# Attention on TensorE: the products with the values of unit u-3 issued ahead of the turning of unit u-2

## The reference, cut to what matters

```python
s_c = jnp.einsum('bqhgd,bnhd->bhgqn', qc, kc).astype(jnp.float32) + head_bias(dist_c)
p_c = masked_softmax(s_c, dist_c >= 0)
o_c = jnp.einsum('bhgqn,bnhd->bqhgd', p_c.astype(vc.dtype), vc)
...
p_s = masked_softmax(...)
o_s = jnp.einsum('bhgqnk,bhqnkd->bqhgd', p_s.astype(v_sel.dtype), v_sel)
...
p_w = masked_softmax(s_w, mask_w)
o_w = jnp.einsum('bhgqk,bkhd->bqhgd', p_w.astype(vwc.dtype), vwc)
return gc[..., 0:1] * o_c + gc[..., 1:2] * o_s + gc[..., 2:3] * o_w
```

## Time and profile before

| | us |
|---|---|
| median of 3 runs (1825.06 to 1826.18) | 1825.11 |
| the profiled execution's own time | 1823.85 |
| its span in the profile | 1821.1 |
| attention, from its first scores to the copy of its last tile | 189.90 to about 280.3 |
| TensorE busy over the span | 1739.9 (96%) |

### The profile page before, as it was taken

How to read it: one execution, slowest core, us unless ns; L and a number is a source line. 1 busy time by engine, 2 the same in 40 slices (tenths; PEclk the granted TensorE clock), 3 DMA queues, 4 the chain that set the end, 5 groups by cost and what they waited for, 6 DMA issues and landing times.

```text
span 1821.1 us, 36387 instructions
## 1 busy us (share of the span) xinstructions
PE 1739.9 (96%) x15582; PEld 1289.7 (71%) x15582; DVE 981.6 (54%) x2058; ACT 497.6 (27%) x1175; POOL 469.8 (26%) x482
## 2 busy tenths in 40 slices
PE   7999899999999999999999979989899999999997
PEld 3446564688888888844555448888867888888886
DVE  4570561444444422323332467666686799999443
ACT  3021682211111100134112544444333222222000
POOL 2060341010111100012000045555453255555100
PEclk9999999999999999999999989999999999999999
DMA  6521102343333343432412100000022222222231
GB/s 236 176 70 47 70 2 98 123 166 123 117 128 117 127 139 118 139 104 91 153 46 76 47 2 5 4 4 5 5 99 70 81 83 91 93 83 84 94 102 55
DMA packets 44760, 158.04 MB, mean 87 GB/s; under 512 B 5112, under 2 KB 7816, under 8 KB 43576
## 3 DMA queue, kind: packets, MB, share of 16 engines
q1 hardware_dynamic: 38304, 132.14, 22.2%
q10 hardware_dynamic: 6296, 23.58, 3.4%
HBM read 150.96 MB, written 6.31 MB: 86 GB/s over the span
## 4 chain that ended last, share of the span: by engine, by line
PE 89%; DVE 6%; ACT 2%; issue 1%; POOL 1%; DMA 0%; SPq 0%; DVEq 0%; ACTq 0%; POOLq 0%
PE psum L364 19%; PE psum L1441 15%; PE psum L1617 15%; PE psum L3083 14%; PE psum L1301 3%; PE psum L2381 2%; PE psum L2954 2%; PE psum L2385 2%; PE psum L691 2%; DVE mem L2571 1%; PE psum L1250 1%; PE psum L1101 1%; PE psum L1074 1%; PE psum L1089 1%; DVE mem L2599 1%
## 5 line engine op out<-in xcount | busy, mean ns | idle before, releaser
L364 PE MATMUL psum<-mem 128*128 128x512 f32 (+1 forms) x880 | 350.3, 556 | 12.3 <-DMA mem<-in_units 11.0
L364 PEld LDWEIGHTS psum<-mem 128*128 128x128 f32 x880 | 165.8, 190 | 184.9 <-issue 178.6
L1441 PE MATMUL psum<-mem 128*128 128x256 f32 x1232 | 272.5, 380 | 1.2 <-issue 1.2
L1617 PE MATMUL psum<-mem 128*128 128x256 f32 x1232 | 269.7, 379 | 0.0
L1441 PEld LDWEIGHTS psum<-mem 128*128 128x128 f32 x1232 | 231.2, 189 | 38.5 <-issue 6.3
L1617 PEld LDWEIGHTS psum<-mem 128*128 128x128 f32 x1232 | 232.1, 189 | 35.0 <-issue 2.4
L3083 PE MATMUL psum<-mem 128*128 128x256 f32 x1176 | 254.4, 379 | 0.0
L3083 PEld LDWEIGHTS psum<-mem 128*128 128x128 f32 x1176 | 221.9, 189 | 32.8 <-issue 0.5
L3208 DVE SCALAR_TENSOR_TENSOR mem<-psum,mem 128x441 f32<-128x441 f32 (+2 forms) x352 | 215.5, 680 | 0.0
L1368 POOL TENSOR_TENSOR mem<-mem 128x256 f32<-128x256 f32 x22 | 16.7, 757 | 281.9 <-DVE mem L1576 271.0
L2381 PE MATMUL psum<-mem 64*64 64x64 f32 x1920 | 75.0, 224 | 13.0 <-DVE mem L2599 5.4
(11 more groups left out here) (387 smaller groups left out, 2426.0 us busy)
## 6 DMA issues: line engine op xcount, KB each, us to landing
mem<-in_units SPq DMA_DIRECT2D x246, 512.0 KB, 3.5
mem<-in_cw ACTq DMA_DIRECT2D x2, 2048.0 KB, 11.2
mem<-in_wn ACTq DMA_DIRECT2D x1, 2048.0 KB, 9.1
bias_tiles<-bias_scratch ACTq DMA_DIRECT2D x1, 2048.0 KB
mem<-bias_tiles ACTq DMA_DIRECT2D x1, 2048.0 KB
mem<-in_xT ACTq DMA_DIRECT2D x1, 2048.0 KB, 9.4
x_scratch<-mem ACTq DMA_DIRECT2D x1, 2048.0 KB, 8.9
mem<-x_scratch ACTq DMA_DIRECT2D x1, 2048.0 KB, 10.5
```

What stands on the lines that cost most here:

```text
L364: last = pe.matmul(dst, w[:, k, :], rhs(k), start=(k == 0), stop=(k == 7))
L1441: last = eng.matmul(dst, w[:, k, :], rhs(k), start=start and k == 0, stop=stop and k == 3, skip_group_check=True)
L1617: ins = eng.matmul(dst, w[:, k, :], rhs(k0 + k), start=opens and first and k == 0, stop=closes and last_ and k == k1 - k0 - 1, skip_group_ ...
```

## The change

TensorE's loop over the units issues the same instructions. Only `weigh(u - 3)` and `turn(u - 2)` have changed places:

```diff
@@ -1108,10 +1108,10 @@
                 for u in range(NU + 3):
                     if u < NU:
                         scores(u)
+                    if u >= 3:
+                        weigh(u - 3)
                     if 2 <= u < NU + 2:
                         turn(u - 2)
-                    if u >= 3:
-                        weigh(u - 3)
```

## The result

Over 20 runs each, the changed kernel takes 1827.34 us (1824.08 to 1832.36) and the kernel before 1824.94 (1820.84 to 1827.43): a ratio of 1.0013, 95% interval 1.0007 to 1.0018. The profiled execution took 1827.13 us.

The account below looks back on a forecast made before the run. TensorE bounds the stage, busy 82.0 of 89.8 us; stretch terms sum to +0.33 us, so span 1821.1 + 0.3 = 1821.4, profiled 1824.2, plus 1.26 gives 1825.5 median; range 1824.4 to 1827.2, wider 1823.6 to 1828.0.

Parts of the forecast that it names:

- GpSimd ceases to hold TensorE in i = 3, 2 and 1: Turnings in these tiles: 1.03 us more time in i = 3 removes the 0.16 us wait for GpSimd every second unit.
- The copy comes on a closed way: Each unit: turning, ScalarE's copy, weigh, next turning set the pace, 3.27 us in i = 3 against TensorE's own 3.11.
- The crossings between tiles: Turnings 8 to 11, 17 to 20 and 26 to 29: changes of -0.17, -0.74 and +0.16 us.
- Rival 1: Whole stage: scores cover the copy and TensorE runs at its own pace, 5.2 us faster, 1819.9; chance 0.05.
- units 29 to 35: Turnings in the last tile, i = 0: 8.5 us against 8.23 before, +0.27, bounds 7.92 to 8.83.
- Rival 2: Wide units: TensorE's switch from weigh to turn dearer than any seen, each 0.1 us costing 3.2 us; chance 0.07.
- The sum: Whole stage: the stretches' changes together give +0.33 us, with bounds of -0.25 to +0.66.
- units 20 to 26: Turnings in i = 1: 12.1 us against 12.20 before, -0.1.
- the six-unit stretches of i = 3 and i = 2: Turnings 2 to 8 and 11 to 17: 19.62 and 15.72 us, +0.68 and +0.27 against before.
- Rival 3: A half-clock stretch falls into the stage (+1.7 us) or the one behind it is missed (-1.7); chance 0.1, split evenly.
- The clock at the stage's end: Half clock for 3.35 us just behind the stage, costing 1.7 us; such a stretch could fall into the stage as well.
- The sign that failed: In the changed trace, the stage was to end within 1 us of 280.3.

Follow-up runs that it names:

- e1: Changed kernel with the turning signalled once per head, so ScalarE copies the low head while TensorE turns the high one: 1820.42 us, ratio 0.9965 to before.
- e3: Changed kernel with one more ScalarE copy of a bank to unused memory in each unit: 1839.86 us, ratio 1.0068 to before.
- e9: Changed kernel with two unused products added in TensorE's wait ahead of its first turning: 1826.97 us, ratio 1.0015 to before.
- e2: Kernel before with the turning signalled once per head instead of once per unit: 1823.23 us, ratio 0.9987 to before.
- e4: Kernel before with one more ScalarE copy of a bank to unused memory in each unit: 1827.58 us, ratio 1.0009 to before.
- e7: Kernel before with only weigh(0) moved ahead of the turning, every later weigh as before: 1824.09 us, ratio 1.0004 to before.
- e11: Same as e1, but VectorE scales both heads in i = 0 and GpSimd none: 1821.97 us, ratio 0.9991 to before.
- e8: Changed kernel from weigh(1) on, with weigh(0) left behind turn(1) as before: 1826.39 us, ratio 1.0012 to before.
- e6: Kernel before with five unused products added in TensorE's wait ahead of its first turning: 1826.30 us, ratio 1.0011 to before.
- e5: Changed kernel with five unused products added in TensorE's wait ahead of its first turning: 1828.09 us, ratio 1.0023 to before.
- e10: Kernel before with two unused products added in TensorE's wait ahead of its first turning: 1824.97 us, ratio 1.0005 to before.
- e12: Same as e11 with two unused products added in TensorE's wait ahead of its first turning: 1819.37 us, ratio 0.9978 to before.

## Why the prediction was right, and where it was off

- **GpSimd ceases to hold TensorE in i = 3, 2 and 1.** Right but for one turning: as a releaser it went from every second unit to two waits of 0.5 us in all, one in i = 1 and one in i = 0.
- **The copy comes on a closed way.** Right, shown by e1 and e3 from both sides. The ways predicted were 3.27, 2.62, 1.98 and 1.32 us; turnings stand 3.29, 2.64 and 1.99 apart and, where nothing else held them, 1.33 (271.92 to 273.25 us).
- **The crossings between tiles.** 8.13, 6.63 and 5.9 us predicted, 8.16, 6.65 and 5.88 measured.
- **Rival 1, the copy is covered.** It does not hold for the change as made, but it does with the signal per head: e1's stage of 85.94 is 3.8 us shorter than before. The 5.2 us that the rival reckoned were too much, since units 29 to 35 took 8.42 us in e1 and not 6.96; also, the prediction compared 3.16 with 3.11 in i = 3, though two of the six rounds there have shorter scores, and e1 went through them in 18.44 us, 3.07 each.
- **Rival 2, the switch from weigh to turn.** Its price is that of the others: 1.04 us for the 16 records of the products, up to the turning, against 1.03 up to the scores before:

```profile
206.89 1.10 PE L1101 MATMUL psum<-mem 128*64 128x128 f32 x16
207.93 1.09 PE L1089 MATMUL psum<-mem 128*128 128x128 f32 x8
```

- **The sum was too small.** I had +0.33 us; the stretches measure +1.28: +1.10 behind turning 2, and at the start +0.18 at full clock (e9, 12.07 against 11.89). The term most mis-sized is units 29 to 35, taken as 8.5 and measured as 8.92, above even its upper bound of 8.83. The other differences are 0.25 for units 20 to 26 and 0.12 and 0.11 for the six-unit stretches of i = 3 and i = 2.

The chain after, at the start of i = 1, and the turning behind it show what the terms for units 20 to 26 and 29 to 35 lack:

```profile
253.73 0.65 ACT mem L1191 x2
254.38 0.49 ACT mem L1196
254.87 0.98 ACT mem L1183 x4
255.85 0.55 ACT mem L1191 x2
...
257.03 0.89 PE L1089 MATMUL psum<-mem 128*128 128x128 f32 x4
```

ScalarE copies the finished tile (L1196) between a unit's copies and the exponentials of a later one, so these exponentials come late, and with them GpSimd's scaling. In i = 1 it ends at 257.42, and the turning at 257.03 lasts 0.89 in place of 0.66 us. In i = 0 the next unit's copies come late as well (a round of 1.70 us from 273.25 in place of 1.33), and the turning behind, at 274.95, lasts 0.70 in place of 0.44. Two more, at 277.88 and 280.69, last 0.59. Together these are the 0.94 us by which units 29 to 35 exceed six times 1.33. The prediction let that copy delay only the last tile, and did not see that behind it GpSimd's waits come back.

- **Rival 3, the clock.** In the changed kernel's trace it came, at the start of the stage: 12.07 us at full clock, 14.43 with a stretch at 0.50 (1.2 GHz), so 2.4 us in place of the 1.7 reckoned. The stretch behind the stage was not missed: it stood at 0.50 from 284.20 to 287.60. The low stretch is not a product of the new order: it stands in the profiled executions of after, e2, e3, e4, e7 and e11, and not in those of before, e1 and e8, nor in the five with added products. But the orders bear it differently. In the order of before, e2's low stretch of 3.4 us left turning 2 at 11.89, for TensorE has slack there while GpSimd scales for 1.86 us. In e4 it lasted 6.8 us, as in the changed kernel's trace, and turning 2 came 1.2 us later; TensorE ran without a wait from 196.62 to that turning at 203.31, so e4's added copy has no part in it. In the changed order weigh(0) stands in the slack and takes 1.9 us in place of 1.03, and the 6.8 us of low clock cost 2.4.
- **The clock at the stage's end.** It was named as a place where a low stretch could fall, and it did: the low stretch around the end lasted 3.4 us in the traces of before, after, e1, e4 and e6, 6.8 us in e3, e5, e8, e9 and e11, and was absent in e2, e7, e10 and e12. So of the five traces with the changed order and one signal for a unit four had the long one, and none of the six with the order of before behind turning 2 had it. In e3, e5, e8, e9 and e11 it began before the stage ended; in e9 this cost 0.25 us inside the stage.
- **The sign that failed.** The stage was to end within 1 us of 280.3. The last copy's end is at 284.21 in the changed kernel's trace, 3.9 us later: 0.3 because it began later, 2.4 by the clock, 1.3 by waits. The other signs came: the products waited for L1191 in nearly every unit, and the turnings stood as far apart as reckoned.

So 1.3 of the 2.4 us are shown to be waits, from the table and e9; this is also the lower end of the measured interval of 1.3 to 3.3. The other 1.1 us are not clear of noise. That the low clock makes them up on average fits the traces, at the start (an estimate: six traces of nine, times 2.4 less the 0 to 1.2 that it costs the order of before, is 0.8 to 1.6 us) or around the end. The medians of e9 and e10 did not show the first, and the mean granted clocks of their executions, 0.9923 and 0.9925, do not show the second. It stays open. The median of 1827.34 lies just above the forecast's own range of 1824.4 to 1827.2 and within the wider one of 1823.6 to 1828.0, which took in the clock. So the small loss and the closed way were foreseen, while the size was held by the width of the range: the waits came out 0.95 us above the sum, and the clock had been given a chance of only 0.1.

## What to carry to other kernels

Before moving work ahead of a wait on one engine, look at what it stood behind: the products that were moved into one wait had been the cover of another, and a transfer between engines that is covered twice by 1.03 and 1.06 us showed no cost here, and covered once 0.18 us every unit in i = 3 (3.29 against 3.11). Write down each closed way (engine, hand-over, engine, back to the first) with its durations and compare it with the engine's own sum; the longest set the pace here, and it was foretold within 0.02 us. Look also for what interrupts such a way only now and then: the copy of a finished tile, once in nine units, is where the sum was furthest off. When a reorder makes a hand-over critical, cut the hand-over as well: a signal for each half turned a loss of 0.13% into a gain of 0.35% (each against its own runs of before; the stage in e1's trace alone gives 3.8 us, 0.21%).

## What the runs showed of the hardware that was not expected

- Around TensorE's 2.3 us of waiting at the stage's start, between 0.8 us before its end and 0.7 us behind it, the granted clock fell to 0.50 in six of nine profiled executions, in either order, for 3.4 us (e2, e7) or 6.8 us (after, e3, e4, e11); where added products lay in the wait it stayed at 1.00 in all five (e5, e6, e9, e10, e12).
- From one execution to the next the clock of the whole matters: over 21 executions of before on one chip, a mean granted clock higher by 0.001 went with a time shorter by 1.4 us, over 35 on another by 1.3, over 35 on a third by 1.0.
- A float32 product of 128 x 512 over all 128 rows took 0.88 us (two records of 0.44, e5), and over 64 rows 0.53, its share of the switch included (the scores' 1.06 for two such products). Reckoning the one by the other spoilt e5 and e6.
